# Chunks 12 to 17 of each layer's input projection: from plain f32 matmuls to three rounded passes

## What is computed

```python
for l in range(DEPTH):
    h = rmsnorm(x, norm_mix_g[l])
    z = h @ w_in[l]
    z_a, z_b, z_c, z_dz, z_dxbc, z_ddt, z_g = split_cols(z, IN_SPLITS)
    y_a = mixer_spatial_gating(z_a, ...)
    y_b = mixer_pool(z_b, ...)
    y_c = mixer_rwkv7(z_c, ...)
    y_d = mixer_ssd(z_dz, z_dxbc, z_ddt, ...)
    ...
    x = x + merged @ w_out[l]
    h = rmsnorm(x, norm_ffn_g[l])
    x = x + (swiglu(h, ...) if l % 2 == 0 else moe_swiglu(h, ...))
```

## Time and profile before

| | us |
|---|---|
| median of 3 runs | 2201.36 |
| lowest and highest | 2195.17 and 2203.12 |
| the profiled execution | 2201.18 |
| its span, first to last instruction | 2199.4 |
| mean granted TensorE clock in it | 0.981 |

### The profile page before, as it was taken

One profiled execution on the slowest core, in us unless ns is written; L12 is line 12 of the kernel. 1 busy time (PEld: TensorE's weight loads), 2 busy tenths in 40 slices (PEclk: granted clock), 3 DMA queues, 4 the chain that ended last, 5 costly groups with the idle time before them and its releaser, 6 DMA issues.

```text
span 2199.4 us, 33003 instructions
## 1 busy us (share of the span) xinstructions
PE 2128.1 (97%) x13016; PEld 1773.7 (81%) x13016; DVE 1537.5 (70%) x1483; ACT 1175.8 (53%) x1033; POOL 52.6 (2%) x56
## 2 busy tenths in 40 slices
PE   8998999989999999999988999999999999999998
PEld 7888999989998988899875777777777777777775
DVE  3668653665544648754547888888888888888886
ACT  4435322533334426322425767776777776777774
POOL 0200000000000020000000000000000000000000
PEclk9999999999999999999978999999999999999999
DMA  7433222545554433222325989999898999899894
GB/s 284 173 107 124 78 77 73 194 152 178 187 192 154 173 115 135 78 77 77 131 81 193 366 339 355 349 347 360 332 367 329 366 348 345 346 349 365 327 368 163
DMA packets 70749, 503.34 MB, mean 229 GB/s; under 512 B 8320, under 2 KB 8576, under 8 KB 9984
## 3 DMA queue, kind: packets, MB, share of 16 engines
q1 hardware_dynamic: 69792, 499.03, 60.6%
q10 hardware_dynamic: 864, 2.95, 0.3%
HBM read 500.90 MB, written 1.05 MB: 228 GB/s over the span
## 4 chain that ended last, share of the span: by engine, by line
PE 93%; DVE 5%; ACT 1%; issue 1%; DMA 0%; DVEq 0%; SPq 0%; ACTq 0%
PE g L485 59%; PE m L485 31%; DVE ring_low L1837 1%; PE m L529 1%; PE m L1014 1%; DVE arena L1673 1%; DVE arena L1671 0%; DVE h L1519 0%; DVE rstd L1517 0%; DVE arena L1755 0%; DVE arena L1753 0%; DVE arena L1760 0%; DVE y_low L1846 0%; DVE rstd L1621 0%; DMA x<-x_in 0%
## 5 line engine op out<-in xcount | busy, mean ns | idle before, releaser
L1978 DVE TENSOR_TENSOR ring_low<-ring,we_high 128x2048 fp32r<-128x2048 f32 x336 | 769.1, 2290 | 153.0 <-ACT we_high L1365 152.8
L1365 ACT ACTIVATE we_high<-ring 128x2048 fp32r<-128x2048 f32 x336 | 644.1, 1918 | 273.6 <-PE g L485 180.5
L485 PE MATMUL g<-we_high,hg_high 128*96 128x512 f32 x896 | 359.7, 401 | 10.3 <-DVE ring_low L1978 10.3
L485 PE MATMUL g<-h_high,ring_low 128*128 128x256 f32 x1248 | 355.2, 285 | 0.0
L485 PE MATMUL g<-we_high,hg_low 128*96 128x512 f32 x896 | 353.5, 394 | 0.0
L485 PE MATMUL g<-ring_low,hg_high 128*96 128x512 f32 x896 | 353.0, 394 | 0.0
L485 PE MATMUL m<-arena 128*128 128x128 f32 (+7 forms) x1824 | 233.5, 295 | 9.9 <-DVE arena L1753 5.9
L485 PEld LDWEIGHTS g<-h_high,ring_low 128*128 128x128 f32 x1248 | 238.7, 191 | 0.0
L485 PEld LDWEIGHTS m<-arena 128*128 128x128 f32 (+3 forms) x1824 | 209.3, 187 | 25.6 <-issue 16.4
L485 PE MATMUL g<-h_high,w_high 128*128 128x256 f32 x736 | 208.3, 283 | 6.8 <-DVE h L1519 6.8
L485 PE MATMUL g<-h_low,w_high 128*128 128x256 f32 x736 | 208.2, 283 | 0.0
(11 more groups left out here) (284 smaller groups left out, 3179.5 us busy)
## 6 DMA issues: line engine op xcount, KB each, us to landing
ring<-stream SPq DMA_DIRECT2D x472, 1024.0 KB, 4.8
sw<-sw_in SPq DMA_DIRECT2D x1, 1088.0 KB, 11.5
sw<-sw_in ACTq DMA_DIRECT2D x1, 1088.0 KB, 7.8
x<-x_in SPq DMA_DIRECT2D x4, 256.0 KB, 5.2
out<-h ACTq DMA_DIRECT2D x4, 256.0 KB, 2.1
cc<-cc_in SPq DMA_DIRECT2D x1, 816.5 KB, 12.6
rep<-rep_in SPq DMA_DIRECT2D x1, 768.0 KB, 13.7
rep<-rep_in ACTq DMA_DIRECT2D x1, 768.0 KB, 7.3
```

Source lines behind the costliest of these rows:

```text
L485: return pe.matmul(o, a, b, start=start, stop=stop, skip_group_check=True)
L1365: A(we_high[n % 3][:, :], ring[:, slot, :], ACT.Copy).then_inc(high_ready, 1)
L1978: TT(ring_low[:, slot, :], ring[:, slot, :], we_high[n % 3][:, :], ALU.subtract).then_inc(low_ready, 1)
```

## The change

Chunks 12 to 17 are split too; 18 stays plain. Their rounded copies go into a new buffer `c_w` of two slots of their own (12, 14 and 16 in slot 1; 13, 15 and 17 in slot 0). ACT gets `c_high(n)`, one copy of 128x2048, at six places in each layer; it waits for the chunk to have landed and, from 13 on, for chunk n - 2 to be used. DVE gets `c_low(n)`, one subtraction of 128x2048, at six places; it waits for `c_high(n)`. PE waits for `c_low(n)` and runs 48 fp32r matmuls instead of 16 plain ones. `c_w` shares memory with the second slot of `w_high` and with `z_w`, the buffer of the next stage, hence the wait for chunk 17 in `z_highs`.

```diff
+            def rounded(l, n):
+                pe.wait_ge(c_low_ready, l * (C_TO - C_FROM) + n - C_FROM + 1)
+                return (c_w[:, 1 - n % 2, :].rearrange("p (b m) -> p b m", b=BLK),
+                        ring_low[:, (chunk0(l) + n) % RING, :].rearrange("p (b m) -> p b m", b=BLK))
...
+            def c_high(l, n):
+                c = chunk0(l) + n
+                act.wait_ge(landed[c % RING], 16 * (c // RING + 1))
+                if n > C_FROM:
+                    act.wait_ge(chunks_used, c - 1)
+                A(c_w[:, 1 - n % 2, :], ring[:, c % RING, :], ACT.Copy).then_inc(c_high_ready, 1)
...
+            def c_low(l, n):
+                dve.wait_ge(c_high_ready, l * (C_TO - C_FROM) + n - C_FROM + 1)
+                TT(ring_low[:, (chunk0(l) + n) % RING, :], ring[:, (chunk0(l) + n) % RING, :], c_w[:, 1 - n % 2, :], ALU.subtract)\
+                    .then_inc(c_low_ready, 1)
...
                 mixer_d_dt(l)
+                c_high(l, 12)
                 evacuate(l, Z_UNITS[10:12])
+                c_high(l, 13)
                 mixer_d(l)
...
-                evacuate(l, Z_UNITS[12:14])
+                evacuate(l, Z_UNITS[12:13])
+                c_high(l, 14)
+                evacuate(l, Z_UNITS[13:14])
+                c_high(l, 15)
...
-                evacuate(l, Z_UNITS[14:16])
+                evacuate(l, Z_UNITS[14:15])
+                c_high(l, 16)
+                evacuate(l, Z_UNITS[15:16])
+                c_high(l, 17)
...
+                if upto == N_SLOTS:
+                    act.wait_ge(chunks_used, chunk0(l) + C_TO)
...
                         filled(dve, l, "yd0")
...
                 for c in range(NCH):
                     filled(dve, l, f"yd{c}")
+                    if c == 0:
+                        c_low(l, 17)
```

More of the change, by code:

```diff
@@ L59 @@
 NS = 11
+C_FROM, C_TO = 12, 18
 N_SLOTS = 5
@@ L233, in trunk @@
         z_w = part("z_w", 25192, [N_SLOTS, HALF])
+        c_w = part("c_w", 26216, [2, CW])
         zc = tiles(4096, CT, T + 1)
@@ L343, in trunk @@
         half_used = sem("half_used")
+        c_high_ready = sem("c_high_ready")
+        c_low_ready = sem("c_low_ready")
         z_high_ready = sem("z_high_ready")
@@ L542, in project @@
                         high = w_high[:, n % 2, :].rearrange("p (b m) -> p b m", b=BLK)
+                    elif C_FROM <= n < C_TO:
+                        high, low = rounded(l, n)
                     else:
@@ L572, in project @@
                                 o = gb((name, i))[:, j * T:(j + 1) * T]
-                                if split:
+                                if split or C_FROM <= n < C_TO:
                                     last = three(o, high[:, DT * j + k, :], low[:, DT * j + k, :], h_high[:, k, :], h_low[k // 4][:, k % 4, :],
@@ L621, in project_quarter @@
                     g_free(pe, l, unit)
-                w = chunk(chunk0(l) + n)
+                high, low = rounded(l, n)
                 for k in range(4 * (part % 2), 4 * (part % 2) + 4):
-                    last = mm(gb(unit)[:, half * T:(half + 1) * T], w[:, DT * half + k, :], h[:, k, :], k == 0, k == DT - 1)
+                    last = three(gb(unit)[:, half * T:(half + 1) * T], high[:, DT * half + k, :], low[:, DT * half + k, :],
+                                 h_high[:, k, :], h_low[k // 4][:, k % 4, :], k == 0, k == DT - 1)
                 if part == 3:
@@ L1564, in mixer_d @@
                 drain("dtT", V.tensor_copy(area(17256, 32), mb("dtT")[:, 0:32]))
+                c_low(l, 14)
                 m_done(dve, l, "dtT")
@@ L1582, in mixer_d @@
                                         ALU.subtract))
+                c_low(l, 15)
                 m_done(dve, l, "row3")
@@ L1604, in mixer_d @@
                             q.step(ins, S["csc_ready"] if g else None)
+                        c_low(l, 16)
                         filled(dve, l, "yd0")
@@ L2071, in _ @@
                 mixer_d_conv(l)
+                c_low(l, 12)
                 mixer_d_decay(l)
+                c_low(l, 13)
                 mixer_a(l)
```

## The result

The changed kernel takes 2213.97 us (median of 6 runs, 2211.57 to 2217.42) against 2197.72 in the 6 runs of the kernel before beside it: a ratio of 1.007, 95% interval 1.0054 to 1.0086. It is slower, by about as much as the ceiling of the gain (14.4 us); the forecast was 2199.6 with a range up to 2206. The profiled execution took 2211.64 us with a span of 2209.9, and its mean granted clock is 0.971 where it was 0.981.

A forecast was written before the change was run, and what follows sets the result against it. PE was taken as the bound, 93% of the span. From 2201.2 us profiled, 4.6 came off for two layers and 3.0 was added for slow clock stretches: 2199.6 us, range 2193 to 2206.

The forecast's parts named there:

- the ceiling of the gain: Six converted chunks save PE 7.2 us a layer, 14.4 us in all; reaching it (2186.8) had chance 0.05.
- The pace of a split chunk: Chunks 12 to 17 on PE: 5.7 us each instead of 6.9, saving 1.2 us a chunk.
- the plan of the DVE queue: Subtractions for chunks 12, 13, 16, 17 mostly hidden; chunk 14's delays the first row, chunk 15's makes PE wait 2.5 us.
- the forecast -2.3 us a layer: Per layer, 2.3 us of the 7.2 saved on PE remain after copies and subtractions; -4.6 us for two layers.
- The POOL term: Rival: chunk 13's subtraction waits for a POOL pooling instruction, delaying mixer A and first row 1.5 us; 2202.6 us, chance 0.10.
- The clock term: After the longer new PE idle piece, before the first row, one half-speed stretch of 3.4 us a layer; +3.0 us in all.
- precedents: Three earlier PE idle pieces: two of 2.28 us followed by 3.4 us at half clock, one of 3.03 us not.
- the range's end of 2206: Upper end of the forecast range: both clock stretches in each layer and POOL's delay together.
- No copy hidden: Rival: all 12 subtractions, 2.3 us each, stand on PE's path, 27.6 us against 14.4 saved; 2214.4 us, chance 0.06.

The follow-up runs named there:

- the first filled kernel: Changed kernel plus extra PE matmuls (10 and 36) in the two idle pieces ahead of the first row product: 2214.4 us, ratio 1.005.
- the filled kernel: Changed kernel plus extra PE matmuls in three idle pieces, 10 and 36 ahead of the first row and 18 ahead of chunk 15: 2202.2 us, ratio 1.0017.
- POOL out of the way: Changed kernel, but POOL starts its pooling only when chunk 14's subtraction is done: 2207.0 us, ratio 1.0037.

## Why the prediction was wrong

**What held.** The pace of a split chunk did: 16 and 17 alone give 2.4 us a layer in the stretch. So did the plan of the DVE queue: mixer A started late, the mask of `cb` came behind it at once (L1599 starts at 101.14, where L1643's successor ended its work at 101.1), chunks 12, 13, 16 and 17 found their subtractions ready, chunk 14's held back the first row, and chunk 15's came late: by 2.20 us at full clock (the first filled kernel), where the forecast had 2.5. In place of the forecast -2.3 us a layer the kernel with PE kept at work has +0.6.

**The POOL term was left out of the sum and mis-sized.** I had it as a rival at 1.5 us a layer and a chance of 0.10. It measured 3.2: L1673 waited 1.33, and chunk 14's subtraction, which I had not put against POOL at all, 1.86. I looked at POOL's row at 92.71 only and not at where its last instruction (2.35 us, at 102.30 before) would stand against the moved DVE. With it, -2.3 becomes +0.9, near the +0.6 of the filled kernel. And the first row came 2.9 us later than before, counted from the last round of the convolution, and 0.3 us earlier with POOL out of the way; the forecast had 0.2 later, so DVE's queue was read well but for POOL. The Trainium skill (SBUF — State Buffer, SBUF: two separate sides) has the one that issues second fully blocked until the other's instruction is through; the traces agree: 4.14 us is the 1.99 until POOL ends at 104.50, and 2.15.

**The clock term was the failed step.** "Between the bounds of nothing and two stretches a layer (3.4) I take one", at 3.4 us of low clock and 1.5 us of cost: it measured 27.3 us in each layer, and 9.3 us of cost. I took the length of a fall from precedents behind which PE went on with dense three-pass products (after 206 us) and used it where PE goes on with row products of 8 partitions, 1.05 us in every 2.7. The trace of before had a warning that I saw and left out: the fall at 352.6 us, 10 us long, begins in a run of small products (64x64 and 128x64) without any idle time and goes on through the three-pass products behind them. So two stretches of 3.4 us were no upper bound, and the range's end of 2206 was wrong with them.

The precedents were also read too narrowly. I put the falls at 206 and 885 down to the idle pieces of 2.28 us ahead of them. With these pieces filled the falls are still there, behind the eight products of 8 partitions that stand in between. The work as well as the idle time ahead of a stretch has to be priced; how the two combine is not known.

**The two terms feed each other.** The 3.2 us from POOL lengthen the gap, and the run without them has 13.7 us of low clock instead of 27.3: 6.5 us a layer go with them, twice their own length. I had added rivals that act on each other.

By the terms: -2.3 forecast, +2.9 (the filled kernel's +0.6 less the forecast) for POOL and whatever else DVE's queue had wrong, +9.3 for the clock is +9.9 a layer, the 72.7 - 62.8 measured.

**A number that agrees by chance.** The rival "No copy hidden" has 2214.4, 0.4 us from the measured median. Its mechanism is not what happened: with the clock at 1.00 the same copies and subtractions cost 0.6 us a layer, not 6.6.

**What stays open.** The sum of the stretches is 19.8 us, the difference of the medians 13 to 16. Part of the rest goes with falls of the clock elsewhere that come, go and change length from trace to trace (353, 172, 844, 858 us); not all of it, since behind the second stretch the changed kernel is 3.9 us shorter with almost the same time at 0.50 (62.6 us, before 63.6). Several kernels have runs in two groups, which may have the same reason, but each kernel has one profile; what the runs of the other group look like inside was not seen. Why one idle piece of 1.94 us is followed by a fall and another, of 1.98 in the trace of before, is not, is not settled either. In the kernel with all but chunk 14 split, the same piece of 1.94 us has no fall behind it in the first layer and one of 10 us in the second.

## What to carry to other kernels

Before adding a wait ahead of light matmuls, ask what the clock will do behind it: a gap of 3.03 us ahead of dense products cost no fall here, one of 3.08 us ahead of the row products 3.4 to 17 us at half speed, and one of 4.94 us up to 27. Falls came behind light products without any gap, too. Where light products stand between the quarters, moving them from plain f32 to three passes went with a longer fall behind the same gap. What helped in the stretch was to put the light work in one piece with the dense work behind it, and to give PE something to do. And when an instruction with two SBUF inputs moves on DVE, lay its new place against POOL's timeline, instruction by instruction.

## What the runs showed of the hardware

- A DVE subtraction of 128x2048 takes 2.29 us, and 4.14 when POOL's 2.34 us instruction was running; 0.69 became 2.02 in the same way. POOL waits too: 1.53 became 3.46.
- The granted clock stayed at 0.50 for 27.3 us in which PE was busy for 23.7 (the changed kernel, both layers), and for 13.7 us with plain quarters in place of split ones.
- It fell without idle time on PE: with at most 0.14 us of it, the clock went to 0.50 for 6.8 and 10.2 us in a run of row products of 8 partitions, and for 3.4 us behind eight such products.
- 64 extra fp32r products a layer (an estimated 7.6 us of PE work, at 5.7 / 48 = 0.119 us each) in three idle pieces made the changed kernel 12 us faster.
